# Two transformer blocks on one core: a first stage with eight weight slots, and reciprocal roots by Ln and Exp

## The reference

```
block 1:
  shift_m, scale_m, gate_m, shift_f, scale_f, gate_f = split(silu(c) @ w_ada + b_ada)   # 6 x 2048
  h = rms_norm(x, g_pre_mix) * (1 + scale_m) + shift_m
  z = h @ w_in                  # 3920 columns: MLA latents, rope key, GLA q k v, gate, r
  o = concat(mla(z...), gla(z...)) @ w_out
  x = x + gate_m * rms_norm(o, g_post_mix)
  h = rms_norm(x, g_pre_ffn) * (1 + scale_f) + shift_f
  x = x + gate_f * rms_norm((silu(h @ w_ffn_gate) * (h @ w_ffn_up)) @ w_ffn_down, g_post_ffn)
mla: c_q, c_kv normalised by rms_norm (512 and 256 wide), rotary angles from positions, 8 heads
gla: 4 heads, gated linear attention in chunks of 64; rms_norm(o, g_gla) * silu(r) per head
block 2: 16 meta rows ahead, forgetting attention, differential attention, a causal convolution
  with silu(layernorm(u)), then a gated feed-forward with a convolution
```

## Time and profile before

| | us |
|---|---|
| median of 3 runs | 2568.98 |
| lowest and highest | 2568.09, 2570.93 |
| profiled execution | 2561.06 |
| its span in the trace | 2559.3 |
| PE busy in it | 2382.4 |
| mean granted PE clock | 0.958 of full |

### The profile page before, as it was taken

One profiled execution on the slowest core, in us unless ns is written; L12 is line 12 of the kernel. 1 busy time (PEld: TensorE's weight loads), 2 busy tenths in 40 slices (PEclk: granted clock), 3 DMA queues, 4 the chain that ended last, 5 costly groups with the idle time before them and its releaser, 6 DMA issues.

```text
span 2559.3 us, 42365 instructions
## 1 busy us (share of the span) xinstructions
PE 2382.4 (93%) x16570; PEld 2222.4 (87%) x16570; DVE 1546.4 (60%) x1735; ACT 1079.8 (42%) x1255; POOL 134.6 (5%) x248
## 2 busy tenths in 40 slices
PE   6989976989999999999989999997999999999996
PEld 6879855789999889997779997697999988999985
DVE  3778769865454457754464896445555644556545
ACT  3343453354444334443444534445444433344333
POOL 0000002300000100001210000000000011000011
PEclk9899987989999999999989999598999999999998
DMA  8978826945555568764545552053555555555552
GB/s 314 348 289 321 293 103 264 377 142 187 181 187 190 192 218 280 272 237 167 180 148 169 175 174 93 1 192 106 181 181 181 179 185 193 181 181 180 182 181 96
DMA packets 163093, 505.28 MB, mean 197 GB/s; under 512 B 8126, under 2 KB 12510, under 8 KB 134062
## 3 DMA queue, kind: packets, MB, share of 16 engines
q1 hardware_dynamic: 161248, 496.66, 56.2%
q0 software_dynamic: 752, 3.47, 0.5%
q10 hardware_dynamic: 1008, 4.00, 0.4%
HBM read 502.00 MB, written 2.10 MB: 197 GB/s over the span
## 4 chain that ended last, share of the span: by engine, by line
PE 84%; DVE 8%; ACT 4%; issue 2%; DMA 1%; ACTq 0%; DVEq 0%
PE pb L505 22%; PE pb L491 18%; PE pb L493 18%; PE pb L492 18%; DVE raw L429 2%; DVE wlo L416 1%; PE pb L470 1%; PE pb L471 1%; PE pb L472 1%; DVE x L1475 1%; PE pb L1852 1%; PE pb L603 1%; ACT whi L404 1%; DMA bcol<-b_ada_columns 1%; DMA raw<-w_in 1%
## 5 line engine op out<-in xcount | busy, mean ns | idle before, releaser
L416 DVE TENSOR_TENSOR wlo<-raw,whi 128x1024 fp32r<-128x1024 f32 (+2 forms) x750 | 905.2, 1217 | 813.7 <-ACT whi L404 812.9
L404 ACT ACTIVATE whi<-raw 128x1024 fp32r<-128x1024 f32 (+2 forms) x750 | 781.4, 1051 | 1108.7 <-PE pb L493 718.1
L491 PE MATMUL pb<-xh,whi 128*128 128x256 f32 (+2 forms) x3760 | 1066.7, 284 | 8.5 <-DVE accf L1538 3.2
L492 PE MATMUL pb<-xl,whi 128*128 128x256 f32 (+2 forms) x3760 | 1066.4, 284 | 0.0
L493 PE MATMUL pb<-xh,wlo 128*128 128x256 f32 (+2 forms) x3760 | 1065.8, 283 | 0.0
L491 PEld LDWEIGHTS pb<-xh,whi 128*128 128x128 f32 x3760 | 712.7, 190 | 10.3 <-issue 4.0
L492 PEld LDWEIGHTS pb<-xl,whi 128*128 128x128 f32 x3760 | 713.8, 190 | 0.0
L493 PEld LDWEIGHTS pb<-xh,wlo 128*128 128x128 f32 x3760 | 712.5, 189 | 0.0
L505 PE MATMUL pb<-whi,stg 128*128 128x512 f32 x1664 | 449.5, 391 | 16.1 <-DVE xl L1452 7.9
L505 PEld LDWEIGHTS pb<-whi,stg 128*128 128x128 f32 x1664 | 313.9, 189 | 84.0 <-DVE xl L1452 8.7
L505 PE MATMUL pb<-wlo,stg 128*128 128x512 f32 x832 | 257.9, 391 | 0.0
(11 more groups left out here) (370 smaller groups left out, 1703.2 us busy)
## 6 DMA issues: line engine op xcount, KB each, us to landing
raw<-w_ada SPq DMA_DIRECT2D x96, 1024.0 KB, 6.5
raw<-w_ffn_gate SPq DMA_DIRECT2D x44, 1024.0 KB, 5.2
raw<-w_ffn_up SPq DMA_DIRECT2D x44, 1024.0 KB, 5.2
raw<-w_ffn_down SPq DMA_DIRECT2D x44, 1024.0 KB, 4.7
raw<-w_gate SPq DMA_DIRECT2D x44, 1024.0 KB, 5.2
raw<-w_up SPq DMA_DIRECT2D x44, 1024.0 KB, 5.1
raw<-w_down SPq DMA_DIRECT2D x44, 1024.0 KB, 4.8
raw<-w_in SPq DMA_DIRECT2D x40, 1024.0 KB, 5.0
```

Of the source, the lines that this page charges most:

```text
L404: act.activation(to, src, ACT.Copy).then_inc(hi_ready, 1)
L416: dve.tensor_tensor(to, src, hi, ALU.subtract).then_inc(raw_done, 1)
L491: mm(o, whi[:, s, t], xh[:, k, c0:c1], start=(k == 0), stop=False)
L492: mm(o, whi[:, s, t], xl[:, k, c0:c1], start=False, stop=False)
```

## The change

- `WIN_PARTS`, `IN_A`, `w_in_row`: a row of the first stage has 16 tiles (2000 columns) instead of 14 (1744); the second stage has four chunks of 4, 4, 4 and 3 tiles instead of 17 tiles. A part of the last chunk is 3 tiles wide, and its unit is padded to 1 MB.
- The first stage's loads go to eight slots (`slots1`): the four of `raw`, the two halves of `xs`, `sigc` and a new `more`. `first_slots` orders them; `sigc` is used once silu(c) is made, the two halves of `xs` once x is transposed.
- All 32 scale and shift columns are sums on DVE; `gemv` and `ON_PE` are gone. The 24 sums of the row stage are spread 2, 2, 1, 2, 2, 1, ... behind rows 0 to 13.
- SP waits for c before its first load; x and the constants are loaded by SP behind two units; positions and b_ada columns come first on ACT's queue. The frequencies travel with the b_ada columns.
- x's rows are scaled on ACT (`Copy` with a scale) instead of DVE.
- `dve_angles` is the first thing on DVE, 13 operations instead of 20.
- `act_tables` comes after `part_hi(3)` instead of before it; `dve_latents` behind part 9 instead of 6.
- The roots of latents, GLA heads and layer norm are Ln, then Exp with scale -0.5, both on ACT; DVE's reciprocals are gone.

```diff
-AHEAD = 4
-ON_PE = (0, 1, 2, 3, 6, 9, 12)
+IN_A = C_QG + GRANK + 9 * P
+HALF_A = (C_QG + GRANK + P, 8 * P)
+AHEAD = 4
+BEHIND_ROW = (2, 2, 1, 2, 2, 1, 2, 2, 1, 2, 2, 1, 2, 2, 0, 0)
...
+    sums = [(kind, t) for t in range(KT) for kind in ("scale", "shift")]
+    units, n = sums[:2 * AHEAD], 2 * AHEAD
     for k in range(KT):
+        units += [("row", k)] + sums[n:n + BEHIND_ROW[k]]
+        n += BEHIND_ROW[k]
...
+EARLY_SLOTS = (0, 1, 2, 3, 6, 7)
+MORE_AT = 10
...
+        if u < len(EARLY_SLOTS):
+            slots.append(EARLY_SLOTS[u])
+        elif u < MORE_AT:
+            slots.append(slots[u - len(EARLY_SLOTS)])
+        elif u < MORE_AT + 2:
+            slots.append(4 + u - MORE_AT)
+        else:
+            slots.append(slots[u - 8])
...
+    slots1 = [raw[:, n, :] for n in range(RING)] + [xs[:, 0, :], xs[:, 1, :], sigc[:, :], more[:, :]]
...
@@ SP
+        sp.wait_ge(sem("cb_in"), 16)
         for u, (kind, t) in enumerate(FIRST):
+            slot = FIRST_SLOT[u]
+            if slot == 6 and slot_loads(u) == 1:
+                sp.wait_ge(sem("csb_done"), 1)
+            elif u in (MORE_AT, MORE_AT + 1):
+                sp.wait_ge(sem("turned"), KT)
+            at_least(sp, raw_done, 2 * slot_before(u, slot))
...
+            sp.dma_start(to, src).then_inc(first_in[slot], 16)
+            if u == 1:
+                for t in range(NT):
+                    sp.dma_start(x[:, t, :], a["x"][0, t * P:(t + 1) * P, :]).then_inc(sem(f"x{t}_in"), 16)
+                sp.dma_start(kc[:, :], a["shape_constants"]).then_inc(consts_in, 16)
@@ ACT
-        for k in range(KT):
+        row_hi(0)
+        for t in range(AHEAD):
+            modulate(t)
+        for k in range(1, KT):
             row_hi(k)
-            if k == 0:
-                for t in range(AHEAD):
-                    modulate(t)
-            if k + AHEAD < KT:
-                modulate(k + AHEAD)
+            for t in tiles_behind(k - 1):
+                modulate(t)
...
         part_hi(2)
-        act_tables()
...
+            for n in range(4 * c + 3, min(4 * c + 5, 16)):
+                part_hi(n)
+                if n == 3:
+                    act_tables()
@@ DVE
+        dve_angles()
         dve.wait_ge(sem("csig"), 1)
...
+        for t in range(AHEAD):
+            first_sum("scale", t)
+            if t in (1, 2):
+                x_rstd(t - 1)
+            first_sum("shift", t)
+        ready = list(range(AHEAD))
         for k in range(KT):
             row_lo(k)
+            n = 2 * AHEAD + sum(BEHIND_ROW[:k])
+            for m in range(n, n + BEHIND_ROW[k]):
+                first_sum(("scale", "shift")[m % 2], m // 2)
+                if m == n:
+                    for t in ready:
+                        x_rest(t)
+                    ready = []
+            for t in ready:
                 x_rest(t)
+            ready = tiles_behind(k)
@@ roots
-            act.activation(zT[:, 20 + h % 2, :], pb[:, h % 2, 0:SEQ], ACT.Sqrt, scale=1.0 / DV, bias=eps)\
-               .then_inc(sem("g_rt"), 1)
+            rt = zT[:, 20 + h % 2, :]
+            act_link(act.activation(rt, pb[:, h % 2, 0:SEQ], ACT.Ln, scale=1.0 / DV, bias=eps))
+            act.activation(rt, rt, ACT.Exp, scale=-0.5).then_inc(sem("g_rt"), 1)
...
-            dve_link(dve.reciprocal(rt, rt))
```

More of the change, by code:

```diff
@@ L89 @@
 W_WINB = W_WIN + 2 * KT
-W_UQ = W_WINB + 34
+W_UQ = W_WINB + 32
 W_UK = W_UQ + 8
@@ L133, with tiles_behind @@
+    assert n == len(sums)
+    return units
+def tiles_behind(k):
+    n = 2 * AHEAD + sum(BEHIND_ROW[:k])
+    return [t for t in range(KT) if n <= 2 * t + 1 < n + BEHIND_ROW[k]]
 FIRST = first_units()
 FIRST_AT = {item: u for u, item in enumerate(FIRST)}
[L137 to L150, removed]
-    for k in range(KT):
[L152 to L155, removed]
@@ L158, with first_slots, slot_loads @@
-FIRST_DONE = first_done()
+EARLY_SLOTS = (0, 1, 2, 3, 6, 7)
+MORE_AT = 10
+def first_slots():
+    slots = []
+    for u in range(len(FIRST)):
+        if u < len(EARLY_SLOTS):
[6 more added lines that the diff above has]
+            slots.append(slots[u - 8])
+    return slots
+FIRST_SLOT = first_slots()
+def slot_loads(u):
+    return FIRST_SLOT[:u + 1].count(FIRST_SLOT[u])
@@ L161, with slot_before @@
+def slot_before(u, slot):
+    return max([v + 1 for v in range(min(u, len(FIRST))) if FIRST_SLOT[v] == slot], default=0)
 ADA_AT = [3 * m + 2 for m in range(4)]
@@ L224, in ada_units @@
             units[n] = part.reshape(KT, P, D)
-    for t in ON_PE:
-        units[0, t] = w[:, t * P:(t + 1) * P].reshape(KT, P, P).transpose(1, 0, 2).reshape(P, D)
     return units.reshape(6 * D, D)
 def w_in_units(w):
-    first = np.concatenate([w[:, 0:C_QG], w[:, C_AG:C_RG], w[:, C_QG:C_QG + 7 * P]], axis=1)
+    first = np.concatenate([w[:, 0:C_QG], w[:, C_AG:C_RG], w[:, C_QG:C_W2]], axis=1)
     second = []
@@ L236, in w_in_units @@
         part = np.concatenate([w[:, c:c + n] for c, n in parts], axis=1)
-        second.append(part.reshape(4, 4, P, CW).transpose(0, 2, 1, 3).reshape(4 * P, D))
-    second.append(w[:, IN1 - P:IN1].reshape(KT, P, P).transpose(1, 0, 2).reshape(P, D))
+        n = part.shape[1]
+        unit = part.reshape(4, 4, P, n).transpose(0, 2, 1, 3).reshape(4 * P, 4 * n)
+        second.append(np.pad(unit, ((0, 0), (0, D - 4 * n))))
     return np.ascontiguousarray(first), np.concatenate(second)
@@ L447, in w_in_row, with w_in_chunk @@
         for n in range(6):
-            tile(s0, n // 2, n % 2, n * P)
-        if k:
-            tile(s0, 3, 1, 6 * P, ROPE + GRANK).then_inc(used, 1)
-        pe.wait_ge(raw_done, done)
-        tile(s1, 3, 0, 0)
-        if k == 0:
[L454 to L459, removed]
+            last = tile(s0, n, n * P)
+            if k == KT - 1 and n in (3, 5):
+                last.then_inc(sem("row_end"), 1)
+        tile(s0, 6, 6 * P + ROPE + GRANK)
+        tile(s0, 7, 6 * P, ROPE + GRANK).then_inc(used, 1)
+        pe.wait_ge(raw_done, done)
+        for n in range(8, 16):
+            last = tile(s1, n, (n - 8) * P)
+        last.then_inc(used, 1)
+    def w_in_chunk(u, w, b0, nf, behind=None):
         for h in range(8):
@@ L2127, in _, with x_rstd @@
[L2127 to L2138 removed]
+        def x_rstd(t):
+            dve.wait_ge(sem("rms"), RMS_AT[0] + t + 1)
+            dve.reciprocal(rstd[:, 0, t:t + 1], stat[:, 0, t:t + 1]).then_inc(sem("x_rstd"), 1)
@@ L2157, in _ @@
+            if n == 9:
                 dve_latents()
             ada_add(U_WIN + 2 * n + 1, adaA, csil[:, n:n + 1])
-        for hh in range(2):
-            split_lo(U_WIN + 32, W_WINB + 32 + hh, hh)
         dve_mla()
```

263 lines of the change are left out of this document (105 added, 158 removed).

## The result

| | before | changed |
|---|---|---|
| median of 4 runs, us | 2568.59 | 2532.23 |
| lowest and highest | 2568.09, 2570.93 | 2528.70, 2534.37 |
| profiled execution, and its span | 2561.06, 2559.3 | 2528.70, 2526.9 |

The ratio is 0.9855, with a 95% interval of 0.9838 to 0.9872: 36.4 us less by the medians, 32.4 by the two profiled spans. The forecast was 2525.6, a gain of 43.4.

What follows compares the result with a forecast made beforehand. PE was taken to bound the run (84% of the chain), so only its waits could give time: 40.9 us up to the second stage's end plus 2.5 at the GLA roots, 43.4 off 2568.98, gives 2525.6; range 2508 to 2548.

Steps and rivals of the forecast that it cites:

- The start: Up to PE's first row matmul: it comes at 45.5 us instead of 58.2, and the gemvs vanish.
- A DMA and a DVE bound that are nearly equal: Row stage after row 0: DMA needs 94.1 us, DVE 93.4, hence 6.6 per row; PE's 5.6 is covered.
- the 1.6 wait: Row stage: DVE's wait per row for ACT's split should go, as that split queues behind a modulation with finished sums.
- Rival 1: Row stage: DVE and ACT stay coupled, the 1.62 wait returns in 14 rows; 2541 us named, chance 0.18.
- Rival 2: Loads: DMA does not hold 420 GB/s; at 350 a unit takes 3.0 us, about 2549 us, chance 0.13.
- Rival 4: Row stage: PE's clock falls to its lower level, 4.6 us over the pace per row; about 2600, chance 0.02.
- Rival 5: Row stage: the slots do not help, the queue empties at the transposes; only the start's 13 us stay, 2556, chance 0.03.
- the second stage: Second stage: 98.0 us in total instead of 109.6, ending at 245.0.
- the tables' wait: Second stage, before the latents: PE waits 4.9 us for tables behind part 3's splits, plus 1.7 of clock.
- Rival 3: New waits hide: tables and Ln/Exp cost nothing (9 us), or the roots give 5 more; 2514 us, chance 0.17.
- The layer norm's roots: Second block's layer norm: Ln then Exp changes nothing, with 1 us to either side.
- The roots of the heads: GLA heads: 7.0 us of DVE reciprocals go, ACT gains two table loads per root; 2.5 us net gain.

Runs made afterwards that it cites:

- e6: Changed kernel with 23 DVE sums of the row stage reading only the first half of their unit, loads unchanged; 2530.80 us, ratio 0.9852 to the kernel before.
- e7: Changed kernel with 23 w_ada units loaded only in their first half, DVE making each sum as two halves; 2529.28 us, ratio 0.9846 to the kernel before.
- e3: Changed kernel with ACT's modulations directly behind the row whose sums DVE is making, as before the change; 2544.60 us, ratio 0.9911 to the kernel before.
- e12: The changed kernel run again with no edit; 2531.75 us, ratio 0.9868 to the kernel before.
- e2: Changed kernel with four slots instead of eight for the first stage's loads and no wait for the transposes; 2535.44 us, ratio 0.9869 to the kernel before.
- e5: Changed kernel with both four load slots and ACT's old modulation order; 2546.75 us, ratio 0.9918 to the kernel before.
- e1: Changed kernel with the Sin tables and latents' squares back ahead of part 3's splits on ACT; 2525.40 us, ratio 0.9833 to the kernel before.
- e10: Changed kernel with the tables back ahead of part 3 and the latents' Ln and Exp behind part 6; 2519.72 us, ratio 0.9815 to the kernel before.
- e4: Changed kernel with the GLA heads' roots back to Sqrt on ACT and reciprocal on DVE; 2531.98 us, ratio 0.9864 to the kernel before.
- e8: Changed kernel in which SP's first loads do not wait for c; 2534.66 us, ratio 0.9865 to the kernel before.

## Why the prediction was right or wrong

**The direction and the mechanism of the row stage were right.** The start came out at 45.9 for 45.5, the end at 147.4 for 147. "A DMA and a DVE bound that are nearly equal" is what e6 and e7 show. The order on ACT, on which I relied for the 1.6 wait, is what e3 takes away. Rivals 1, 2, 4 and 5 fall in this profile: ACT's wait did not come back, DMA held 421, the clock was 0.99 in 50 to 130, the queue did not empty at the transposes (it did at the end of the row stage, which no rival named). Rival 5 has something true in it, though: the slots give 7.6 us of the row stage in the profile and nothing clear of noise in the time. One reading of the earlier trace rows was wrong and cost nothing: at 52 to 56 PE was not in the gemvs, which ended at 45.5, but idle (0.00 in the row), while ACT was busy with copies and modulations.

**The step that failed is the second stage, by size.** It had 98.0 and took 103.0 to its end (102.6 as the table counts). Part of this is one execution's clock: e12 took 99.0, and over the nine kernels with this second stage unchanged the mean is 101.1. I saw the tables' wait and priced it at 4.9, from "the second of these may only start when PE has done half 3". That price is what e2 and e5 show, where the last split waited for PE and not for its load. In the changed kernel the split waited for its load, both halves then stood ahead of the tables, and PE waited 6.4 (1.5 more). That DMA "stays under PE's 5.6" a pair is true of the rate, but it took for granted that the first loads of the stage come in time. I allowed 1.7 for clock behind it; the latents' matmuls alone took 6.65 instead of 3.7 (1.2 more). Ahead of chunk 1 came a wait of 1.8 and a clock of 0.66 over 5 us, 3.5 for the 1.7 predicted (1.8 more). These are 4.5 of the 5.0; the rest I can't place. Rival 3's thought, that the tables might hide, was right only of the old place: e1.

**Three things I did not count.** First, from the end of the second stage to the first `w_uq` matmul. The one-tile chunk that the change removes had covered the hand-over (read from the two timelines; no run puts it back): it ran until 285.9 while ACT made three of the four `w_uq` splits, and its copy out was short. ACT and PE of the kernel before, then of the changed one:

```profile
286.95 0.36 ACT L1994 ACTIVATE zT<-pb 128x256 f32<-128x256 f32 x1
...
290.58 0.36 PE L763 MATMUL pb<-xh,whi 128*128 128x256 f32 x1 [1.13 <-issue]
```

```profile
252.48 0.79 ACT L2013 ACTIVATE zT<-pb 128x768 f32<-128x768 f32 x1
...
256.53 0.55 PE L806 MATMUL pb<-xh,whi 128*128 128x256 f32 x1 [2.56 <-issue]
```

From the end of the chunks to the first `w_uq` matmul it was 4.7 (285.85 to 290.58) and is 6.15 (250.38 to 256.53), 1.4 more: the first split of `w_uq` now waits for its load until 248.8, the fourth ends 2.2 behind the last chunk's end, and the copy is 0.79 instead of 0.36. In e12 and e1 it is 7.2 and 6.7. The attention then begins with a lower clock (the first matmuls 0.21 apart, not 0.117; in e10 they are 0.12 apart), and up to the GLA 1.5 more are lost. Second, the Sqrt table at the norm behind `w_out`, 1.15. Third, 1.6 us of clock at 1134 to 1142: PE waits 3.0 us just before in both kernels, behind eight matmuls of 512 columns, and the granted clock then was 0.79 in the changed one and 1.00 in the one before. This is not the change's doing, as far as the profiles tell: e4 has the same wait and 1.00, e12 0.79. The changed kernel, then the one before:

```profile
1133.69:1141.69 8.00, 8.00 (x30) 6.40 (x29) 0.07 (x1) 1.16 (x2) 0.75 (x2) 0.79 0.00 0
```

```profile
1168.00:1176.00 8.00, 8.00 (x37) 6.58 (x36) 1.66 (x2) 2.04 (x3) 0.75 (x2) 1.00 0.01 2
```

**The sum.** By the profiled pair: 35.5 gained up to the end of the second stage (predicted 40.9), less 1.4 and 1.5 to the GLA, plus 2.4 there (predicted 2.5), makes 35.0 at `w_out`; 0.5 more in `w_out`, less 1.15, less 1.6, and small change: 32.4. The layer norm's roots cost nothing, as predicted: from the convolution's start at 1292.03 before (1259.31 after) to its attention's at 1608.30 (1575.54) it is 316.3 and 316.2. The medians show 36.4, so by them the forecast of 43.4 missed by 7.0, not by 11. The difference lies within the spread of single executions, 2528.5 to 2536.1 over the eight of the changed kernel; the profiled execution of the kernel before was 7.5 under its median, that of the changed one 3.5.

**The roots of the heads.** The rows for each root (answers to the earlier trace rows):

```profile
L1192 ACT ACT_TABLE_LOAD  x4: 1283/1283/1283, 353.1 to 375.4; - x4
...
L1193 ACT ACT_TABLE_LOAD  x4: 1283/1283/1283, 355.1 to 378.0; - x4
```

Two loads per root, eight in all, as counted. The Trainium skill, ScalarE: Activation LUTs, section on table sets, has one load for a Ln followed by an Exp; the trace disagrees four times over.

## What to carry to other kernels

When a step is moved behind another one on its queue, price what that other one waits for (here a load), not only its duration, and add the lower clock of the engine that is made to wait: together that was some 7 us for one moved call. Ask too whether the queue of loads is full where one stage hands over to the next. When two resources are at their bound at once, an edit on one of them shows next to nothing (0.3 and 1.6 us here), so cut each in turn before choosing. A short leftover stage that looks like waste can be the cover of the next hand-over, and a change of function on ScalarE can be paid where the next other function runs, here 90 us later.

## What was not expected of the hardware

- The same wait is followed by a lower clock in one execution and not in another, or by a longer stretch of it. Behind PE's 3.0 us wait at 1133 (1167 before) the clock was 0.79 or 1.00 for 8 us. Behind the tables' wait it was at half for some 6 us in the changed kernel (0.51 in the 6 us from 165.29) and for some 4 in e12, the same code (0.50 in the 4 us from 163.68, then 1.00); behind the same wait of 1.8 ahead of chunk 1 it was 0.66 in the one and 1.00 in the other. Of the 3.9 us between their second stages 1.3 is the wait itself and 2.6 the clock. That the 8 us between single runs come from this is likely, not shown.
- A load of 1 MB (c) that is queued beside 1 MB weight loads on another queue takes 16.1 us to land in e8, 8.2 in the kernel before, where it is issued first, and 5.6 in the changed kernel, where the weights wait for it.
- 421 GB/s into one core, held for 122 us.
